# Differential attention: an order of its own for each engine, with scores and maxima two tiles ahead

## The reference

```python
def diff_attention(q, k_sh, v_sh, lq1, lk1, lq2, lk2, subln, lam_init):
    ...
    def block(args):                       # 128 queries, i = 0..7
        q_blk, i = args
        t = i * Q_BLOCK + jnp.arange(Q_BLOCK)
        s = jnp.einsum('bqhcd,bkhcd->bhcqk', q_blk, k, preferred_element_type=jnp.float32)
        dist = jnp.abs(t[:, None] - pos[None, :]).astype(jnp.float32)
        bias = -slopes[:, None, None] * dist
        allowed = (pos[None, :] // CHUNK) <= (t[:, None] // CHUNK)
        s = jnp.where(allowed, s + bias[None, :, None], -jnp.inf)
        p = jax.nn.softmax(s, axis=-1)
        attn = (p[:, :, 0] - lam * p[:, :, 1]).astype(v.dtype)
        return jnp.einsum('bhqk,bkhe->bqhe', attn, v)
    ...
    o = rms_norm_2(o, subln) * (1.0 - lam_init)
    return o.reshape(B, S, BR_W)
```

## Time and profile before

| what | value |
|---|---|
| runs | 2929.01, 2937.88, 9256.51 us |
| median | 2937.88 us |
| profiled execution, its own time | 2937.09 us |
| its span, first to last instruction | 2935.9 us |
| TensorE busy (matmul) | 2726.5 us, 93% |
| VectorE, ScalarE, GpSimd busy | 47%, 32%, 22% |
| mean granted TensorE clock | 0.972 of full |
| HBM traffic over the span | 54 GB/s |

### The profile page before, as it was taken

How to read it: one execution, slowest core, us unless ns; L and a number is a source line. 1 busy time by engine, 2 the same in 40 slices (tenths; PEclk the granted TensorE clock), 3 DMA queues, 4 the chain that set the end, 5 groups by cost and what they waited for, 6 DMA issues and landing times.

```text
span 2935.9 us, 49632 instructions
## 1 busy us (share of the span) xinstructions
PE 2726.5 (93%) x20750; PEld 2191.2 (75%) x20750; DVE 1375.3 (47%) x2528; ACT 926.2 (32%) x1854; POOL 632.1 (22%) x631
## 2 busy tenths in 40 slices
PE   8998979999999999999999997888879999989879
PEld 6785667888888887778788865878747778766657
DVE  4236674333333333452455306777654332366652
ACT  3226743211111111243122122444453122144541
POOL 1003243111111111234211101222113201134340
PEclk9999989999999999999999996999989999999999
DMA  3121041112111111111211210000023201123232
GB/s 123 48 72 37 16 137 58 37 58 58 50 44 51 51 43 51 51 58 62 76 37 37 68 60 1 4 32 4 4 94 115 72 22 46 29 57 62 66 84 115
DMA packets 161438, 160.33 MB, mean 55 GB/s; under 512 B 9152, under 2 KB 134714, under 8 KB 159682
## 3 DMA queue, kind: packets, MB, share of 16 engines
q1 hardware_dynamic: 161218, 157.17, 17.7%
HBM read 135.07 MB, written 22.08 MB: 54 GB/s over the span
## 4 chain that ended last, share of the span: by engine, by line
PE 79%; DVE 7%; ACT 4%; DMA 3%; POOL 3%; issue 3%; SPq 0%; DVEq 0%; ACTq 0%; POOLq 0%
PE ps L935 13%; PE ps L937 13%; PE ps L936 13%; PE ps L2520 7%; PE ps L990 5%; PE ps L992 5%; PE ps L991 5%; PE ps L1817 2%; PE ps L1563 2%; PE ps L1564 2%; PE ps L1565 2%; DMA sb<-in_w_ffn_gate 1%; PE ps L1895 1%; DVE r L900 1%; PE ps L1913 1%
## 5 line engine op out<-in xcount | busy, mean ns | idle before, releaser
L935 PE MATMUL ps<-r,r 128*128 128x512 f32 (+1 forms) x1760 | 700.0, 398 | 7.1 <-DVE sb L1274 4.4
L937 PE MATMUL ps<-r,r 128*128 128x512 f32 (+1 forms) x1760 | 685.2, 389 | 0.0
L936 PE MATMUL ps<-r,r 128*128 128x512 f32 (+1 forms) x1760 | 685.1, 389 | 0.0
L881 POOL TENSOR_TENSOR sb<-sb 128x1024 f32<-128x1024 f32 x117 | 231.4, 1987 | 1222.2 <-DMA sb<-in_w_ffn_up 482.7
L935 PEld LDWEIGHTS ps<-r,r 128*128 128x128 f32 x1760 | 332.7, 189 | 99.0 <-issue 25.3
L937 PEld LDWEIGHTS ps<-r,r 128*128 128x128 f32 x1760 | 332.7, 189 | 69.1
L936 PEld LDWEIGHTS ps<-r,r 128*128 128x128 f32 x1760 | 333.0, 189 | 65.3 <-issue 1.7
L900 DVE TENSOR_TENSOR r<-sb,r 128x1024 fp32r<-128x1024 f32 x182 | 235.7, 1312 | 309.3 <-ACT r L895 309.1
L990 PE MATMUL ps<-r,r 128*128 128x512 f32 (+1 forms) x768 | 303.8, 396 | 41.0 <-DVE r L900 16.9
L2520 PE MATMUL ps<-sb 64*64 64x64 f16 (+2 forms) x8832 | 270.2, 216 | 32.4 <-issue 11.4
L992 PE MATMUL ps<-r,r 128*128 128x512 f32 (+1 forms) x768 | 296.2, 386 | 0.0
(11 more groups left out here) (266 smaller groups left out, 3401.0 us busy)
## 6 DMA issues: line engine op xcount, KB each, us to landing
sb<-in_a_w_in SPq DMA_DIRECT2D x29, 512.0 KB, 4.0
sb<-in_w_out SPq DMA_DIRECT2D x24, 512.0 KB, 5.7
sb<-in_w_ffn_gate SPq DMA_DIRECT2D x22, 512.0 KB, 4.6
sb<-in_w_ffn_up SPq DMA_DIRECT2D x22, 512.0 KB, 3.9
sb<-in_w_ffn_down SPq DMA_DIRECT2D x22, 512.0 KB, 3.4
sb<-in_w_in SPq DMA_DIRECT2D x17, 512.0 KB, 4.4
xs<-sb SPq DMA_DIRECT2D x4, 2048.0 KB, 7.0
gates<-sb SPq DMA_DIRECT2D x32, 256.0 KB, 2.0
```

The costliest lines, as they stand in the source:

```text
L881: pool.tensor_tensor(w.raw, w.raw, w.gain.unsqueeze(2).broadcast_to((P, w.nk, w.n)), ALU.mult).then_inc(*s.w_gain.up(w.id))
L935: pe.matmul(self.out, w.hi[:, q, self.cols], hi, start=(q == 0), stop=False)
L936: pe.matmul(self.out, w.hi[:, q, self.cols], lo, start=False, stop=False)
L937: ins = pe.matmul(self.out, w.lo[:, q, self.cols], hi, start=False, stop=(q == w.nk - 1))
```

## The change

`Attention.steps` no longer writes one list for all engines but one string for each, in `ORDER_PAIRS`. A letter is a step (C scores, M0 and M1 the masked maximum of map 0 or 1, X0 and X1 the exponential, N combination, U0 and U1 the two groups of transposes, W values, O, Q, K, Z the pair's norm, G a place of fills); the number is how many tiles ahead of t it is made. TensorE now makes the scores of tile t+2 first in tile t. VectorE makes the maximum of map 1 of tile t+2 ahead of the fills of places 0 to 2 and that of map 0 behind them. ScalarE makes the exponential of map 1 of tile t+1 early in tile t, that of map 0 behind the copies, and every fill's part after that. GpSimd and SP have their fills behind the pair's steps. `Alone` gets the weights of a fill for its TensorE part, so that `with_weights` finds it there: Load, Gain and Round stand by the TensorE entries, which come first in a tile. The steps themselves, their instructions and their waits are unchanged.

```diff
--- before.py
+++ after.py
@@ -1664,34 +1664,35 @@
     def buf(self, iq, h):
         return (2 * iq + h) % 4
 
+    ORDER_PAIRS = {
+        "pe": "C:2 G:0 G:1 U0:0 G:2 U1:0 W:0 Q:-1 G:3",
+        "dve": "N:0 O:-1 K:-2 M1:2 G:0 G:1 G:2 M0:2 G:3",
+        "act": "O:-1 X1:1 U0:0 U1:0 X0:1 G:0 G:1 G:2 G:3",
+        "pool": "Q:-1 K:-2 Z:-3 G:0 G:1 G:2 G:3",
+        "sp": "K:-2 G:0 G:1 G:2 G:3",
+    }
+
     def steps(self, fill, beside):
 
-
-        part = lambda kind, t, *more: [kind(self.k, self, *divmod(t, ST), *more)]
         last = self.n * ST - 1
-        out = part(Scores, 0) + part(Biased, 0) + part(Exponentials, 0)
-        for t in range(last + 1):
-            out += part(Normalise, t)
-            if t and t % 2 == 0:
-                out += part(PairOut, t - 1)
-            if t > 2 and t % 2:
-                out += part(PairMean, t - 2)
-            if t < last:
-                out += part(Scores, t + 1) + part(Biased, t + 1)
-            out += fill(t, 0) + fill(t, 1)
-            for n in range(len(self.groups(*divmod(t, ST)))):
-                out += part(Turned, t, n)
-                if n == 0:
-                    out += fill(t, 2)
-            if t % 2:
-                out += part(PairValues, t)
-            if t < last:
-                out += part(Exponentials, t + 1)
-            if t and t % 2 == 0:
-                out += part(PairSum, t - 1)
-            if t > 3 and t % 2 == 0:
-                out += part(PairScale, t - 3)
-            out += fill(t, 3) + beside.get(t, [])
+        kinds = {"C": (Scores,), "M0": (Biased, (0,)), "M1": (Biased, (1,)), "X0": (Exponentials, (0,)), "X1": (Exponentials, (1,)), "N": (Normalise,),
+                 "U0": (Turned, 0), "U1": (Turned, 1), "W": (PairValues,), "O": (PairOut,), "Q": (PairSum,), "K": (PairMean,), "Z": (PairScale,)}
+        made, out = {}, []
+        for t in range(-2, last + 1):
+            fills = [fill(t, place) for place in range(4)]
+            for engine, names in self.ORDER_PAIRS.items():
+                for name, ahead in (word.split(":") for word in names.split()):
+                    if name == "G":
+                        out += [Alone(self.k, step, engine) for step in fills[int(ahead)]]
+                        continue
+                    at = t + int(ahead)
+                    if not 0 <= at <= last or name == "U1" and at % ST < 4 or name in "WOQKZ" and at % 2 == 0:
+                        continue
+                    if (name, at) not in made:
+                        kind, *more = kinds[name]
+                        made[name, at] = kind(self.k, self, *divmod(at, ST), *more)
+                    out.append(Alone(self.k, made[name, at], engine))
+            out += beside.get(t, [])
         return out
 
     ORDER = {
@@ -1769,6 +1770,12 @@
     def __init__(self, k, step, engine):
         super().__init__(k)
         self.step, self.engine = step, engine
+        if engine == "pe":
+            self.weights, self.paces = step.weights, step.paces
+
+    def plan(self):
+        if self.engine == "pe":
+            self.step.plan()
 
     def sp(self, sp):
         if self.engine == "sp":
```

## The result

Before: 2936.03 us, median of 4 runs (2929.01, 2934.18, 2937.88 and one far off, 9256.51). After: 2968.93 us, median of 4 (2967.01 to 2975.42). The ratio is 1.0129, 95% interval 1.0111 to 1.0146: slower, by 33 us going by the medians and by 38 going by the ratio, which leaves the far-off run out; not the 4 to 5 us forecast, and outside the range. The profiled execution of the changed kernel has a span of 2966.0 us where the kernel before had 2935.9.

A forecast was written before the change was run, and what follows sets the result against it. TensorE, busy over 90%, idles about 34 us in this stage; after the change GpSimd's pair loop binds. TensorE's 3 to 4 us gain doesn't reach the end, the loop ends 4.5 us later: 2937.1+4.5 = 2941.6, given as 2941; range 2927 to 2954.

The forecast's parts named there:

- Weight rounding: Cast and subtraction now precede VectorE's combination; costed at nothing under 5 to 6 us of cover, else up to 2.4 us each.
- TensorE's waits: Idle time in a full head: 1.1+1.1+1.0 = 3.2 us where 4.2 was, 1 us saved in each of four heads.
- New wait 1: At tile 4, scores wait for map 0's maximum, itself behind the last transposes: TensorE idles 1.1 us, replacing 0.84 us.
- New wait 2: A product's copy on VectorE stands in front of map 0's maximum, delaying the scores: 1.1 us idle, once per head.
- tile 7's: Wait before tile 7's transposes: 2.08 us less 1.2 for one exponential, plus 0.3 of the maximum's wait, leaving 1.0 us.
- the gap at L1274: TensorE's wait for the copy out of bank 7, now behind one maximum instead of two: 1.08 us falls to nothing.
- The term at the start: At the stage's start, a second set of scores waits for two maxima of 256 columns before any fill: 1.2 us.
- The charge for the shared port pair: VectorE combinations meeting GpSimd's gating more often: ten up to 1 us longer, taking away TensorE's 3 us gain.
- The loop's side: GpSimd's per-pair round trip through DRAM becomes the bound, 47.5 us per 46.5 us head; rounds of 10.0, end 4.5 us later.
- The gating behind the scaling: On GpSimd, a product's gating, 2.7 us, moves from the loop's shadow into it: eight of 18 rounds, 21.4 us.
- Rival 3: Slower by coupling: VectorE's PairMean waits for GpSimd's square, stopping TensorE too, once lag passes 10.9 us: 2954 us, chance 0.12.
- Rival 1: The order works and the loop keeps up, so TensorE's 3 to 4 us, or up to 15, come through: 2928 us, chance 0.18.

The follow-up runs named there:

- Run 12: Changed kernel with casts and subtractions at the end of ScalarE's and VectorE's part of the tile, Load and Gain still at its head: 2948.71 us, 1.0043.
- run 2: Old orders for all engines, written as strings, with Load, Gain and Round moved to the head of the tile: 2958.47 us, 1.0096.
- run 5: Old orders as strings, Round back behind the maxima, only Load and Gain at the head of the tile: 2948.26 us, 1.0045.
- Run 8: Changed kernel with 25 added matmuls in front of TensorE's wait for the combination at six tiles: 2963.08 us, 1.0104.
- Run 9: New orders of TensorE, VectorE and ScalarE alone; GpSimd's order and SP's list as in the kernel before, weight steps back within the tile: 2947.33 us, 1.0033.
- run 13: Control: old orders as strings, all weight steps back; eight neighbouring pairs on VectorE and ScalarE differ from the kernel before: 2946.39 us, 1.0032.
- run 17: As run 13, subtractions behind the copy of bank 7 (VectorE's list as in the kernel before), casts behind the first copy of transposes: 2946.99 us, 1.0039.
- run 15: As run 9, but TensorE makes the scores of tile t+2 behind the fills of places 0 and 1: 2942.70 us, 1.0017.
- run 18: As run 15, with subtractions behind the copies of bank 7 and casts behind the first copy of transposes: 2944.19 us, 1.0023.
- run 14: Changed kernel with SP's string named first, so Load stands behind the pair's transfers; Gain and Round stay at the head: 2959.45 us, 1.0086.
- Run 4: Kernel before without the factors' write to DRAM and broadcast back, GpSimd multiplying by the gate instead (output not the reference's): 2935.52 us, 1.0012.
- Run 1: Changed kernel with GpSimd's old order (PairMean, fills 0 to 2, PairSum, PairScale, fill 3), all else as changed: 2959.69 us, 1.0093.
- Run 16: Kernel before with 29 added matmuls in front of TensorE's wait for the combination at seven tiles: 2938.36 us, 1.0008.
- run 11: Old orders on all engines, only Load at the head of its tile, Gain and Round where they were: 2951.74 us, 1.0052.

## Why the prediction was wrong

**The step that failed: "Weight rounding ... I cost it at nothing".** Its bound, 2.4 us for each of five tiles, took only the two instructions' own time. What the cast waits for was left out: Gain, behind GpSimd's scalings and the gating, behind the broadcast. At tile 12 VectorE stood in front of the subtraction for 7.46 us, with the combination queued behind it:

```profile
2621.70 1.04 ACT L895 CAST r<-sb 128x1024 fp32r<-128x1024 f32 x1 [6.27 <-POOL sb L881]
2622.78 1.23 DVE L900 TENSOR_TENSOR r<-sb,r 128x1024 fp32r<-128x1024 f32 x1 [7.46 <-ACT r L895]
```

No 5 to 6 us of cover hides that. Run 12 prices the step at 20 us by the medians and 25 by the ratios in the changed kernel (1.0043 against 1.0129), runs 2 and 5 at 10 to 15 us with the old orders (1.0096 against 1.0045). In both comparisons the intervals are clear of each other. I had the parts: the prediction says that Gain moves, that the gating comes behind the scaling, and that Round precedes the combination. I priced each on its own engine and never walked the line across them.

**The clock was no term.** 17.4 of the 36.6 us are the same matmuls, busy for longer at a lower granted clock. The stretches of the earlier trace rows showed 0.96 and 0.93, which could have been asked about. Run 8 shows the clock to follow the waits and to be paid for: with one wait filled a head went from 52.93 to 48.43 us, 3.5 us of it behind that wait. By the Trainium skill (TensorE: Matmul & The Clock Gate, Part 1), the throttled state is the default and activity releases it. The trace agrees: the clock stands at 0.50 from 2623 to 2635 us, in and behind the gap of 5.51 us, and is back at 1.00 with TensorE at work.

**TensorE's waits** were sized well, one by one, where the roundings are out of the way, but the sum missed one. I forecast 3.2 us idle in a full head, made of two waits of 1.1 and one of 1.0. In run 12 the head from 2582.66 has 0.19, 0.86, 0.79, 0.42, 0.99 and 0.80, idle 4.15 us in all. New wait 1 (0.99) and new wait 2 (0.79) are there, and tile 7's is 0.86 of 1.0. But the wait before tile 5's transposes, whose place new wait 1 was to take, is still 0.80 us (0.84 before), and the gap at L1274 shrank to 0.42, where I had nothing. Before, it was 3.5 and 3.6 us of idle in the two heads of this cut without a clock loss, so even this part gains nothing. Run 9 against its controls 13 and 17 (1.0033; 1.0032, 1.0039) says it as a time: this order two tiles ahead is worth nothing either way. With the scores later (runs 15 and 18: 1.0017, 1.0023) it is 0.1 to 0.2% below the controls with intervals that overlap, so a small gain is neither shown nor excluded. The term at the start was right: the waits are 1.22, 0.85 and 1.15 us, where they were 1.19 and 0.90. The charge for the shared port pair didn't come: the 48 combinations took 43.1 us in all before and 41.1 after.

**The loop's side** was wrong in size and in what it binds. From the power of pair 3 to that of pair 21 I forecast 210.5 us; it took 2845.64-2604.98 = 240.7. With the gating and Gain as I counted them, a round is (240.7-21.4-7.6)/18 = 11.8 us, not 10.0. But this is not the loop's own length. Run 12 has the same orders on GpSimd and SP, and there the same two powers begin at 2604.01 and 2825.81, 221.8 us apart, a round of 10.7 us: the upper end of what I had allowed. The other 19 us come back with the roundings. Of what is left one reason has a number: with a Load just ahead the write takes 4.4 to 5.1 us, not 2.7 to 3.8, and I allowed for a Load's wait only, not for its traffic (run 14, with Load behind, is 9 us faster). The premise was wrong too. Run 4 shortens the time from power to scaling by 2 to 7 us in 17 of the 24 rounds of the kernel before (7.2, 5.0, 2.3 and 2.1 us in pairs 18 to 21) and gains nothing, and the stretch from the last head's first scores to the end stays at 157 us. So the last head was not bound by the loop, though the chain of waits runs through it. That other work of about the same length stood next in line is my inference.

**The gating behind the scaling** I charged at 2.68 us in eight rounds, up to 21 us on the loop, 4.5 at the end. Run 1 gives 10 us back for it. The price is of the right kind. That it reaches the end through Gain and the cast, and not through the tail, is what the chain at tile 12 and the casts' shorter wait in run 1 suggest.

**Rival 3, coupling,** had the right idea in the wrong place. I asked only whether VectorE's PairMean would wait for GpSimd's square and set the point at a round of 10.9 us. In the changed kernel that wait doesn't appear; the coupling came through Gain, cast and subtraction. Its 2954 us was the loop's length alone. Rival 1's 2928 us follows from neither of its own terms: 2937 less 3 to 4 is 2933 to 2934, less 15 it is 2922, below the stated range. That had no part in the miss.

**What stays open.** Old orders, written as strings with every weight step back in its place, still take 0.3 to 0.4% more than the kernel before (runs 13 and 17). Their traces show where. In run 17 the heads with tiles 12 and 28 are 7 us longer together, in run 13 10 us: Gain falls on VectorE's small product, a gap of 2.3 to 3.7 us follows at L1274, and half the clock for some microseconds. Another 4 us are in the fifth head of each, which has no such collision; there the wait before tile 34's transposes grew from 1.90 us to 2.53 in run 17 and 3.45 in run 13. What brings the collision about is only argued. The time from pair 3's power to the scaling is 9.68 us in run 17 and 8.60 before; neighbour swaps on ScalarE and ordinary scatter of the transfers could both do that. Run 16, which has no swap at all and has the collision, speaks for the scatter, but its total is that of the kernel before (1.0008), and one trace of each kernel doesn't say how often the collision comes. No run moved Gain alone. So of the 33 us, 20 are shown to be the roundings' place, and the 10 or so that are left are as much as the controls lose too and are not settled.

## What to carry over

- A step that moves to another place in a queue brings along everything that its own inputs wait for. Price it by walking back from it across all engines in the new order, not by its duration; a step that waits for GpSimd or a DMA belongs behind the work that TensorE is waiting for.
- When orders are rewritten, build the control first: the old order in the new form. Here it was 0.3% off, which is more than any effect of two tiles ahead that the runs show.
- Ask of each new gap on TensorE what the granted clock does behind it. Here nearly as much time was lost at the low clock (17.4 us) as in the added gaps (19.2 us).

## What the runs showed of the hardware

- VectorE's product of 128x1 took 1.87 us where it takes 0.22, beside GpSimd's 128x1024 product of 1.89 us, and ended 0.01 us after it. In runs 13 and 16 it took 1.71 and 1.67 us and again ended with Gain, to 0.02 us: not slowed by a share but held until the other's end. The Trainium skill (SBUF — State Buffer, the shared port pair) says that the pair is locked for a whole instruction against a VectorE operation with two SBUF inputs; the rows agree with it. The size of the small operation is no protection.
- From its issue to the issue of the broadcast that waits for it, a write of 1 KB took 4.4 to 5.1 us in the six rounds of the changed kernel in which a load of 512 KB was issued 0.9 to 1.7 us ahead of it, and 2.7 to 3.8 us in the other eighteen. The same shows in run 11 (4.66 us at tile 12).
- TensorE's clock fell to the 1.2 GHz level during one gap of 5.51 us, in the changed kernel; the scores of a 1024-column tile behind it then took 3.79 us, not 1.99. In run 8 it also fell without a long gap, behind two of 1.04 and 1.55 us close together.
